# Forgetting attention: the value product with 64 leading and 64 low columns in one stationary operand

## The chip, the cores and the metric

The kernel runs on one core of one Trainium2 chip. The metric is device microseconds (us) of one execution. TensorE does matrix products and transposes, VectorE (DVE) and ScalarE (ACT) do elementwise work and read PSUM, GpSimd (POOL) does elementwise work in SBUF, SyncE (SP) issues transfers. Each engine works through its own queue in order; semaphores tie the queues together.

## The reference

Two transformer blocks in float32 over 512 tokens (plus 16 meta tokens in the first, plus 256 context tokens in the second). The change touches one piece of the first block, the forgetting attention (8 heads of 64):

```
c = jnp.cumsum(log_f, axis=1)                       # per head
s = q . k / sqrt(64) + (c_i - c_j);  causal mask     # blocks of 128 queries, 528 keys
p = softmax(s)
o = einsum('bhqk,bkhd->bqhd', p, v)                  # the value product
```

In the same block runs a linear recurrence (HGRN2) of 4 heads with 128 keys, evaluated in levels of halved block size; the outputs of both are concatenated and multiplied by `w_out`. Then come a feed-forward network, a block of differential attention, a block of neighbourhood attention, and a feed-forward network behind each.

## The kernel before

Float32 operands go to TensorE in the type float32r, and accuracy is kept by splitting: `hi` is the operand rounded to that type, `lo` the rest, and every product is three, `hi*hi + hi*lo + lo*hi`. The helper `mm3` (lines 367 to 371) issues them; `halve_scalar` (L534, on ACT) writes `hi` from the source and `halve_vector` (L539, on DVE) writes `lo = source - hi` behind it. Weights come in chunks: SP fetches one into `raw`, ACT rounds it to `whi` (`split_hi`, L400), POOL or DVE makes `wlo` (`split_lo`, L411), and TensorE uses it.

The stage that holds the change is "mixers", from about 60 to 373 us of the span. `mixers_steps` is a hand-written list of steps: for each of four rounds j, attention for the pair of heads 2j and 2j+1 and recurrence head j. In a round there are four query blocks i = 0 to 3, each with "scores" and two "turn" steps (transposes of the probabilities, one per head). "values" steps exist for x = 2, 3 (query blocks 0 and 1, head 0 and head 1 of the pair) and x = 6, 7 (blocks 2 and 3): 16 in all. Between them the list is filled with the projections of the next round and with the recurrence ("level", "keys", "states", "output", "sums"). TensorE runs the steps in list order. The orders of ACT, DVE and POOL come from `in_time`: each step has a planned end on TensorE (`mixers_cost`, `mixers_chain`), the tables `MIXERS_SCALAR`, `MIXERS_VECTOR` and `MIXERS_GPSIMD` give each part of a step a lateness against it, and the parts are sorted by the resulting time. `Spare` picks for each result the PSUM bank (4 to 7) planned free first; TensorE waits there for the last reader of the bank's former content.

A "values" step: the stationary operand is `vh` or `vl`, 128 keys by 128 columns (both heads of the pair, 64 each); the moving operand is the transposed probabilities of one head, `th`/`tl` (blocks of keys) and `mh`/`ml` (the 16 meta keys), 256 query columns, 128 in the diagonal block. For x = 2, 3 there are 3 blocks (256, 128 and 256 columns), for x = 6, 7 five (three of 256, one of 128, one of 256). Of the 128 rows that come out, the 64 of the head (rows `r` to `r+63`) are used: ACT rounds them to `foh` ("o_hi"), DVE writes `fol` ("o_lo"), which frees the bank.

ACT's order around x = 6, 7 of round j is: gk_root (L1281, L1283), o_hi 6, o_hi 7, tv_hi of the next round (two pieces), split (L400), decay (L1287), exp (L1229), gv (L1292), t_hi, share (L1235), gv second half (L1292), split, gtv (L1297, L1299), level_exp (L1313). DVE's is: o_lo 6, gk_close (L1460 to L1468, five instructions), o_lo 7, max (L1410), tv_lo, decay_sum (L1473, five scans), inv (L1416), t_lo, diff (L1491, L1492), scaled (L1499, L1500). TensorE transposes the evacuated gv (L1098) behind both halves of L1292, and then runs the level products (L1114).

At the end of the stage, ACT has "close", split, o_hi 6, o_hi 7, DVE has "close", "part" 7 (L1551), o_lo 6, o_lo 7, and `mixed_tensor` begins with a wait on the o_lo of x = 7 and the recurrence's close.

## Time and profile before

| | |
|---|---|
| median of 3 runs | 2616.43 us |
| all three | 2621.54, 2616.43, 2616.13 us |
| span of the profiled execution | 2620.7 us |
| TensorE busy | 2449.5 us, 93% |
| VectorE, ScalarE, GpSimd busy | 1563.9, 1056.3, 345.6 us |
| stage "mixers" | about 60 to 373 us |

The profile comes from one execution, whose own time is known as its span, 2620.7 us from the first to the last instruction; no other figure was taken for it. It lies 4.3 us above the median of the three runs and 0.8 us below the slowest. In the rows below PE is TensorE's products and PEld its weight loads; L534 means line 534 of the kernel before.

### The profile page before, as it was taken

To read this page: it belongs to the slowest core of one execution; us is meant where nothing else is said; L and a number is where in the kernel's file an instruction comes from. 1 tells how busy PE (TensorE), PEld (TensorE's weight loads), DVE (VectorE), ACT (ScalarE), POOL (GpSimd) and SP (SyncE) were. 2 spreads that over 40 slices of the span, in tenths; PEclk is the share of its full clock that TensorE was granted. 3 is DMA by queue.
4 is the path that set the end of the run, shared out by engine and by line. 5 is a ranking of instruction groups with operands and counts; after the bars stand their busy time and mean duration, and the time that the engine had idled before them with its cause. 6 is when DMAs were issued, how large, how long until landed. Compare 5 with 4: busy or idle time off the path is not lost.

```text
span 2620.7 us, 35948 instructions
## 1 busy us (share of the span) xinstructions
PE 2449.5 (93%) x14115; PEld 2107.4 (80%) x14115; DVE 1563.9 (60%) x3020; ACT 1056.3 (40%) x1878; POOL 345.6 (13%) x241
## 2 busy tenths in 40 slices
PE   7999989999998999998899999999889897999998
PEld 6788877788787878776788888889778786888887
DVE  4566657878867777777756544445545456533334
ACT  5455534223254555555521211113555545422223
POOL 2222210000031221221000000002222322000001
PEclk9999999999999999999899999999999999899999
DMA  4222125555521111111234333331212122232331
GB/s 121 61 65 58 47 83 160 174 157 176 175 75 43 41 35 39 41 33 41 73 104 130 104 110 108 119 115 46 53 44 57 45 53 57 76 109 85 100 109 49
DMA packets 240617, 220.73 MB, mean 84 GB/s; under 512 B 26620, under 2 KB 207650, under 8 KB 240450
## 3 DMA queue, kind: packets, MB, share of 16 engines
q1 hardware_dynamic: 240450, 218.45, 27.4%
q8 instruction: 112, 1.84, 0.3%
q14 instruction: 55, 0.45, 0.1%
HBM read 216.17 MB, written 2.24 MB: 83 GB/s over the span
## 4 chain that ended last, share of the span: by engine, by line
PE 73%; DVE 13%; ACT 7%; issue 5%; DMA 1%; SPq 0%; POOL 0%; DVEq 0%; POOLq 0%; ACTq 0%
PE ps L369 23%; PE ps L370 22%; PE ps L371 22%; ACT whi L400 1%; PE ps L2492 1%; DVE FR L539 1%; PE ps L2944 1%; ACT FA L2585 1%; DVE FA L673 1%; DVE hT L2665 1%; ACT FR L534 1%; DVE wlo L411 1%; DVE FA L2705 1%; PE ps L1114 1%; ACT FA L3013 1%
## 5 line engine op out<-in xcount | busy, mean ns | idle before, releaser
L369 PE MATMUL ps<-Uh,whi 128*128 128x512 f32 (+2 forms) x2544 | 898.3, 353 | 17.5 <-ACT FA L2604 5.9
L370 PE MATMUL ps<-Ul,whi 128*128 128x512 f32 (+2 forms) x2544 | 884.5, 348 | 0.0
L371 PE MATMUL ps<-Uh,wlo 128*128 128x512 f32 (+2 forms) x2544 | 883.7, 347 | 0.0
L369 PEld LDWEIGHTS ps<-Uh,whi 128*128 128x128 f32 x2544 | 487.5, 192 | 84.7 <-issue 18.0
L371 PEld LDWEIGHTS ps<-Uh,wlo 128*128 128x128 f32 x2544 | 486.3, 191 | 59.5
L370 PEld LDWEIGHTS ps<-Ul,whi 128*128 128x128 f32 x2544 | 487.2, 192 | 57.0
L400 ACT ACTIVATE whi<-raw 128x1024 fp32r<-128x1024 f32 (+3 forms) x211 | 297.8, 1411 | 539.8 <-PE ps L371 539.6
L411 DVE TENSOR_TENSOR wlo<-raw,whi 128x2048 fp32r<-128x2048 f32 (+2 forms) x117 | 239.3, 2046 | 258.5 <-ACT whi L400 258.1
L369 PE MATMUL ps<-FR,whi 128*128 128x512 f32 (+1 forms) x864 | 302.4, 350 | 14.3 <-DVE FR L539 7.8
L411 POOL TENSOR_TENSOR wlo<-raw,whi 128x1024 fp32r<-128x1024 f32 (+1 forms) x94 | 227.3, 2418 | 666.3 <-ACT whi L400 665.5
L370 PE MATMUL ps<-FR,whi 128*128 128x512 f32 (+1 forms) x864 | 298.6, 346 | 0.0
L371 PE MATMUL ps<-FR,wlo 128*128 128x512 f32 (+1 forms) x864 | 298.3, 345 | 0.0
L539 DVE TENSOR_TENSOR FR<-ps,FR 128x512 fp32r<-128x512 f32 (+7 forms) x284 | 142.6, 534 | 141.5 <-ACT FR L534 140.7
L2185 POOL TENSOR_TENSOR FA<-FA 128x256 f32<-128x256 f32 x63 | 48.5, 787 | 1298.6 <-ACT FA L2065 1297.5
L534 ACT ACTIVATE FR<-FA 128x512 fp32r<-128x512 f32 x100 | 58.4, 584 | 352.1 <-DVE FA L1860 343.5
L673 DVE SCALAR_TENSOR_TENSOR FA<-FA,cond 128x512 f32<-128x512 f32 x280 | 197.0, 745 | 2.6 <-DMA FA<-in_ada_w_dram 1.2
L369 PEld LDWEIGHTS ps<-FR,whi 128*128 128x128 f32 x864 | 164.4, 190 | 38.0 <-issue 9.6
L534 ACT ACTIVATE FR<-ps 128x512 fp32r<-128x512 f32 (+7 forms) x304 | 131.5, 467 | 125.2 <-PE ps L371 74.3
L371 PEld LDWEIGHTS ps<-FR,wlo 128*128 128x128 f32 x864 | 164.3, 190 | 20.0
L370 PEld LDWEIGHTS ps<-FR,whi 128*128 128x128 f32 x864 | 164.5, 190 | 19.3
L369 PE MATMUL ps<-whi 128*128 128x512 f32 (+1 forms) x208 | 86.8, 417 | 47.4 <-DVE hT L3097 28.5
L1860 DVE TENSOR_TENSOR FA<-ps,FA 128x512 f32<-128x512 f32 x88 | 54.9, 623 | 115.9 <-PE ps L371 114.4
(347 smaller groups left out, 2999.2 us busy)
## 6 DMA issues: line engine op xcount, KB each, us to landing
FA<-in_ada_w_dram SPq DMA_DIRECT2D x192, 256.0 KB, 2.8
raw<-in_ffn_w_gate_up_dram SPq DMA_DIRECT2D x44, 1024.0 KB, 5.1
raw<-in_ffn_w_down_dram SPq DMA_DIRECT2D x24, 768.0 KB, 4.6
raw<-in_w_in_dram SPq DMA_DIRECT2D x29, 512.0 KB, 3.9
raw<-in_da_wqkv_dram SPq DMA_DIRECT2D x24, 512.0 KB, 3.7
raw<-in_na_wqkv_dram SPq DMA_DIRECT2D x24, 512.0 KB, 3.8
raw<-in_w_ffn_gate_dram SPq DMA_DIRECT2D x11, 1024.0 KB, 5.4
raw<-in_w_ffn_up_dram SPq DMA_DIRECT2D x11, 1024.0 KB, 5.4
```

The costliest lines, as they stand in the source:

```text
L369: e.matmul(out, ah, bh, start=start, stop=False)
L370: e.matmul(out, ah, bl, start=False, stop=False)
L371: return e.matmul(out, al, bh, start=False, stop=stop)
L400: e.activation(K.view(K.hi[i % 2], i), K.view(K.raw[i % 2], i), ACT.Copy).then_inc(*K.ev("whi", i))
L411: e.tensor_tensor(K.view(K.lo[i % 2], i), K.view(K.raw[i % 2], i), K.view(K.hi[i % 2], i).bitcast(F32), ALU.subtract).then_inc(*K.ev(by, i))
L534: e.activation(hi, src, ACT.Copy, scale=scale).then_inc(*K.ev(*done))
L539: e.tensor_tensor(lo, src, hi.bitcast(F32), ALU.subtract).then_inc(*K.ev(*done))
L673: e.scalar_tensor_tensor(out=o, in0=wv, scalar=K.cond[:, k, c:c + 1], in1=o, op0=ALU.mult, op1=ALU.add).then_inc(*K.ev("ada", i, c))
L1114: t = e.matmul(o[:, c * P:(c + 1) * P], a[:, c * P:(c + 1) * P], b[:, c * P:(c + 1) * P], start=True, stop=True)
L1860: e.tensor_tensor(mt, K.bank(4 + m % 2)[:, 0:t1 - t0], K.sil[:, m % 2, 0:t1 - t0], ALU.mult).then_inc(*K.ev("f_mul", st, m))
L2185: e.tensor_tensor(acc, acc, K.st_sq4[:, k, :], ALU.add).then_inc(*K.ev("pool_sum", f.st, n, i, z))
L2492: t = e.matmul(K.ps[:, 1024 * mp + c0:1024 * mp + c0 + a1 - a0], q[r:r + 64, q0:q0 + P], k[r:r + 64, a0:a1], start=n == 0, stop=n == 2)
```

## The change

The leading and the low part of one head's values stand side by side as one stationary operand of 128 columns (64 and 64), and each block takes two products (with the leading and the low probabilities) instead of three. The rows that come out are 64 sums of the leading values and 64 of the low ones, and they have to be added: ACT copies the low rows to the head's partitions in SBUF ("o_other"), DVE adds the others from PSUM ("o_sum", which now frees the bank), and o_hi and o_lo then read this sum in SBUF. The planned times of o_hi and o_lo move by 1.0 us. `tv_hi` and `tv_lo` write the new layout; `Uh` and `Ul` become halves of one tensor `U` so that one pattern reaches both.

```diff
-        self.fv = self.Uh[:, 0:5, 528:656], self.Ul[:, 0:5, 528:656]
+        zy = self.U[:, :, 528:656].rearrange("p (z y) d -> p z y d", z=2)[:, :, 0:5, :]
+        self.fvw, self.fv = [zy[:, h, :, :] for h in range(2)], (zy[:, :, :, 0:64], zy[:, :, :, 64:128])
+        self.folow, self.fofull = self.hT[:, 0:4, 560:624], self.hT[:, 4:8, 560:624]
...
+def by_64(a):
+    return a.rearrange("p (a b) -> p a b", b=64)
+def by_pair(a):
+    return a.rearrange("p (y h d) -> p h y d", h=2, d=64)
...
-        o = K.hold(w, b, ("x_o_lo", j, x))
+        o = K.hold(w, b, ("x_o_sum", j, x))
...
-            t = mm3(e, o[:, c0:256], vh[0:kn, y, :], vl[0:kn, y, :], ah, al, z == 0, z == len(order) - 1)
+            for m, a in enumerate((th[:, y, c0:256], tl[:, y, c0:256]) if y < 4 else (mh[0:NM, :], ml[0:NM, :])):
+                t = e.matmul(o[:, c0:256], K.fvw[h][0:kn, y, :], a, start=z == 0 and m == 0, stop=z == len(order) - 1 and m == 1)
...
-                 "values": (("o_hi", 0.1),),
+                 "values": (("o_other", 0.1), ("o_hi", 1.1)),
...
-        halve_scalar(K, e, K.bank(K.xbank["tv", j, 0]).rearrange("p (a b) -> p a b", a=4), vh[:, 0:4, :], ("x_tv_hi", j, 0))
+        halve_scalar(K, e, by_pair(K.bank(K.xbank["tv", j, 0])), vh[:, :, 0:4, :], ("x_tv_hi", j, 0))
...
     elif what == "o_hi":
         r, c0 = 64 * (x % 2), (x // 4) * 256
+        w.wait_ge(*K.at("x_o_sum", j, x))
+        halve_scalar(K, e, K.fofull[r:r + 64, :, :], by_64(K.foh[r:r + 64, j, c0:c0 + 256]), ("x_o_hi", j, x))
+    elif what == "o_other":
+        r = 64 * (x % 2)
         w.wait_ge(*K.at("x_values", j, x))
-        halve_scalar(K, e, K.bank(K.xbank["o", j, x])[r:r + 64, 0:256], K.foh[r:r + 64, j, c0:c0 + 256], ("x_o_hi", j, x))
+        n = 4 * j + x // 4 * 2 + x % 2 - 2
+        if n >= 0:
+            w.wait_ge(*K.at("x_o_sum", n // 4, 2 + 4 * (n % 4 // 2) + n % 2))
+        e.activation(K.folow[r:r + 64, :, :], by_64(K.bank(K.xbank["o", j, x])[64 - r:128 - r, 0:256]), ACT.Copy).then_inc(*K.ev("x_o_other", j, x))
...
-                 "turn": (("t_lo", 0.8),), "values": (("o_lo", 0.6),),
+                 "turn": (("t_lo", 0.8),), "values": (("o_sum", 0.6), ("o_lo", 1.6)),
...
+    elif what == "o_sum":
+        r, n = 64 * (x % 2), 4 * j + x // 4 * 2 + x % 2 - 2
+        w.wait_ge(*K.at("x_o_other", j, x))
+        if n >= 0:
+            w.wait_ge(*K.at("x_o_lo", n // 4, 2 + 4 * (n % 4 // 2) + n % 2))
+        e.tensor_tensor(K.fofull[r:r + 64, :, :], by_64(K.bank(K.xbank["o", j, x])[r:r + 64, 0:256]), K.folow[r:r + 64, :, :], ALU.add).then_inc(
+            *K.ev("x_o_sum", j, x))
```

The orders that follow from the new tables, by the sorting of `in_time`: ACT around x = 6, 7: gk_root, o_other 6, o_hi 6, o_other 7, tv_hi, o_hi 7, split, decay. DVE: o_sum 6, gk_close, o_lo 6, o_sum 7, max, o_lo 7, tv_lo, decay_sum. ACT around x = 2, 3 (rounds 0 to 2): o_other 2, share, o_hi 2, o_other 3, t_hi, o_hi 3, split. ACT at the end: close, split, o_other 6, o_hi 6, o_other 7, o_hi 7; DVE: close, part 7, o_sum 6, o_lo 6, o_sum 7, o_lo 7.

## Rows read from the trace of the kernel before

**Rows 1.** Page: the span and the engines' busy time.
```profile
span 2620.7 us, 35948 instructions
PE 2449.5 (93%) x14115; PEld 2107.4 (80%) x14115; DVE 1563.9 (60%) x3020; ACT 1056.3 (40%) x1878; POOL 345.6 (13%) x241
```
**Rows 2.** Waits of TensorE in 60 to 380 us: us in total, times, longest.
```profile
PE ps L1114 <- DVE raw L1500: 7.0, 10, 0.9
```
**Rows 3.** Timeline of TensorE: values 2, 3 of round 0; start, us, instruction.
```profile
109.42 0.28 PE L370 MATMUL ps<-wlo,Uh 128*128 128x256 f32 x1
109.54 0.28 PE L371 MATMUL ps<-whi,Ul 128*128 128x256 f32 x1
...
111.96 0.66 PE L1064 MATMUL ps<-ident,FA 128*128 128x128 f32 x4
```
**Rows 4.** Timeline of TensorE: values 6, 7 of round 3.
```profile
365.20 0.28 PE L369 MATMUL ps<-whi,Uh 128*128 128x256 f32 x1
...
367.19 0.39 PE L369 MATMUL ps<-FR,Uh 128*128 128x256 f32 x1
```
**Rows 5.** Timeline of ACT: around values 2, 3 of round 0.
```profile
110.69 0.38 ACT L534 ACTIVATE FR<-ps 64x256 fp32r<-64x256 f32 x1 [1.58 <-PE ps L371]
110.97 1.35 ACT L1235 ACTIVATE FA<-FA,stat 128x528 f32<-128x528 f32 x2
```
**Rows 6.** Timeline of ACT: around values 6, 7 of round 0.
```profile
145.75 0.38 ACT L534 ACTIVATE FR<-ps 64x256 fp32r<-64x256 f32 x1 [1.26 <-PE ps L371]
146.33 0.75 ACT L534 ACTIVATE Uh<-ps 128x512 fp32r<-128x512 f32 x2 [0.20 <-PE ps L1034]
146.98 1.04 ACT L400 ACTIVATE whi<-raw 128x1024 fp32r<-128x1024 f32 x1
148.06 0.65 ACT L1287 ACTIVATE FA<-raw 128x528 f32<-128x528 f32 x1
...
151.96 0.94 ACT L1235 ACTIVATE FA<-FA,stat 128x272 f32<-128x272 f32 x2 [0.94 <-DVE stat L1416]
153.47 0.39 ACT L1292 ACTIVATE FA<-ps 128x264 f32<-128x264 f32 x1 [0.56 <-PE ps L371]
```
**Rows 7.** Timeline of DVE: the same stretch.
```profile
148.00 0.43 DVE L539 TENSOR_TENSOR FR<-ps,FR 64x256 fp32r<-64x256 f32 x1
...
149.98 1.89 DVE L1473 TENSOR_TENSOR_SCAN FA<-ones,FA 128x128 f32<-128x128 f32 x5
...
156.08 1.54 DVE L1499 TENSOR_TENSOR raw<-raw,FA 128x256 f32<-128x256 f32 x1 [3.04 <-ACT raw L1313]
```
**Rows 8.** Timeline of POOL: the same stretch.
```profile
148.16 2.40 POOL L411 TENSOR_TENSOR wlo<-raw,whi 128x1024 fp32r<-128x1024 f32 x1 [9.19 <-ACT whi L400]
154.95 2.39 POOL L411 TENSOR_TENSOR wlo<-raw,whi 128x1024 fp32r<-128x1024 f32 x1 [4.38 <-ACT whi L400]
```
**Rows 9.** Timeline of TensorE: the transposes of gv behind both halves of L1292.
```profile
153.91 0.66 PE L1098 MATMUL ps<-ident,FA 128*128 128x128 f32 x4 [0.48 <-ACT FA L1292]
```
**Rows 10.** The scans of line 1473: ns min/median/max.
```profile
L1473 DVE TENSOR_TENSOR_SCAN FA<-ones,FA x15: 157/393/860, 150.0 to 301.7; 128x128 f32<-128x128 f32 x12, 128x16 f32<-128x16 f32 x3
```
**Rows 11.** Timeline, all engines: the end of the stage.
```profile
370.88 0.76 ACT L534 ACTIVATE FR<-ps 64x256 fp32r<-64x256 f32 x2
...
371.62 0.68 DVE L1551 TENSOR_TENSOR hT<-ps,hT 128x512 f32<-128x512 f32 x1
...
372.22 0.86 DVE L539 TENSOR_TENSOR FR<-ps,FR 64x256 fp32r<-64x256 f32 x2
...
373.29 0.77 PE L369 MATMUL ps<-FR,whi 128*128 128x512 f32 x1 [3.97 <-DVE FR L539]
```
**Rows 12.** Timeline of TensorE: an idle time of 3.12 us later on.
```profile
395.44 0.47 PE L369 MATMUL ps<-Uh,whi 128*128 128x512 f32 x1 [3.12 <-ACT hT L1674]
```
**Rows 13.** Windows: busy us of PE, PEld, DVE, ACT, POOL; then TensorE's clock.
```profile
396.00:398.00 2.00, 2.00 (x7) 1.62 (x6) 1.93 (x4) 1.54 (x5) 0.00 (x0) 0.62 0.34 117
398.00:400.00 2.00, 2.00 (x6) 1.52 (x6) 1.92 (x3) 2.00 (x3) 0.00 (x0) 0.52 0.00 0
```

More of the change, by code:

```diff
@@ L1075, in fox_tensor @@
             kn = P if y < 4 else NM
-            ah, al = (th[:, y, c0:256], tl[:, y, c0:256]) if y < 4 else (mh[0:NM, :], ml[0:NM, :])
-            t = mm3(e, o[:, c0:256], vh[0:kn, y, :], vl[0:kn, y, :], ah, al, z == 0, z == len(order) - 1)
+            for m, a in enumerate((th[:, y, c0:256], tl[:, y, c0:256]) if y < 4 else (mh[0:NM, :], ml[0:NM, :])):
+                t = e.matmul(o[:, c0:256], K.fvw[h][0:kn, y, :], a, start=z == 0 and m == 0, stop=z == len(order) - 1 and m == 1)
         t.then_inc(*K.ev("x_values", j, x))
@@ L1219, in fox_scalar @@
         w.wait_ge(*K.at("x_tv", j, 0))
-        halve_scalar(K, e, K.bank(K.xbank["tv", j, 0]).rearrange("p (a b) -> p a b", a=4), vh[:, 0:4, :], ("x_tv_hi", j, 0))
+        halve_scalar(K, e, by_pair(K.bank(K.xbank["tv", j, 0])), vh[:, :, 0:4, :], ("x_tv_hi", j, 0))
         w.wait_ge(*K.at("x_tv", j, 1))
-        halve_scalar(K, e, K.bank(K.xbank["tv", j, 1])[0:NM, 0:P], vh[0:NM, 4, :], ("x_tv_hi", j, 1))
+        halve_scalar(K, e, by_pair(K.bank(K.xbank["tv", j, 1])[0:NM, 0:P])[:, :, 0, :], vh[0:NM, :, 4, :], ("x_tv_hi", j, 1))
     elif what == "exp":
@@ L1397, in fox_vector @@
         w.wait_ge(*K.at("x_tv_hi", j, 0))
-        halve_vector(K, e, K.bank(K.xbank["tv", j, 0]).rearrange("p (a b) -> p a b", a=4), vh[:, 0:4, :], vl[:, 0:4, :],
-                     ("x_tv_lo", j, 0))
+        halve_vector(K, e, by_pair(K.bank(K.xbank["tv", j, 0])), vh[:, :, 0:4, :], vl[:, :, 0:4, :], ("x_tv_lo", j, 0))
         w.wait_ge(*K.at("x_tv_hi", j, 1))
-        halve_vector(K, e, K.bank(K.xbank["tv", j, 1])[0:NM, 0:P], vh[0:NM, 4, :], vl[0:NM, 4, :], ("x_tv_lo", j, 1))
+        halve_vector(K, e, by_pair(K.bank(K.xbank["tv", j, 1])[0:NM, 0:P])[:, :, 0, :], vh[0:NM, :, 4, :], vl[0:NM, :, 4, :], ("x_tv_lo", j, 1))
     elif what == "max":
@@ L1434, in fox_vector @@
         w.wait_ge(*K.at("x_o_hi", j, x))
-        halve_vector(K, e, K.bank(K.xbank["o", j, x])[r:r + 64, 0:256], K.foh[r:r + 64, j, c0:c0 + 256],
-                     K.fol[r:r + 64, j, c0:c0 + 256], ("x_o_lo", j, x))
+        halve_vector(K, e, K.fofull[r:r + 64, :, :], by_64(K.foh[r:r + 64, j, c0:c0 + 256]),
+                     by_64(K.fol[r:r + 64, j, c0:c0 + 256]), ("x_o_lo", j, x))
+    elif what == "o_sum":
[5 more added lines that the diff above has]
+            *K.ev("x_o_sum", j, x))
 def hgrn_vector(K, e, w, what, h, n):
@@ L3274, in build @@
         m["hT"] = sb("hT", [P, KC, 768])
-        m["Uh"] = sb("Uh", [P, KC, 768], F32R)
-        m["Ul"] = sb("Ul", [P, KC, 768], F32R)
+        m["U"] = sb("U", [P, 2 * KC, 768], F32R)
+        m["Uh"], m["Ul"] = m["U"][:, 0:KC, :], m["U"][:, KC:2 * KC, :]
         m["FR"] = sb("FR", [P, 13376], F32R)
```

## Prediction

> **What bounds the kernel now.** I read the page first, then the waits of TensorE in the stage that the change touches, then the timelines of each engine around the value products. The page shows TensorE at work for 93% of the span [rows 1]; DVE has 60% and ACT 40%. Taken alone that says that fewer products are less time. In the stage itself, though, TensorE is held up at fixed places: ten times for the recurrence's level inputs from DVE (7.0 us in all, [rows 2]) and in each round for ACT's evacuation of gv [rows 9]. What counts is whether a saved product lies behind such a place or ahead of it, and what the new steps do to the two in-order queues of ACT and DVE.
>
> **What is removed on TensorE.** 16 values steps: eight (x = 2, 3) lose 3 products each, eight (x = 6, 7) lose 5: 64 products. Products of 256 columns start 0.12 us apart [rows 3]: 64 x 0.12 = 7.7 us. From above: a head's whole step of 15 products lasts 1.99 us [rows 4], 0.133 each, 8.5 us for 64. I take 7.7: per pair of steps 0.7 us at x = 2, 3 and 1.2 us at x = 6, 7. The weight loads go with the products, and the two that stay have the same form as before.
>
> **x = 2, 3 (four places).** The new ACT order is o_other 2, share, o_hi 2, o_other 3, t_hi. o_other 2 takes the slot of the old o_hi (0.38 us at 110.69, [rows 5]), 0.35 us earlier; share, which takes 1.35 us for two heads, then starts at about 110.63 instead of 110.97, and its first half is done at 111.3. The next transposes on TensorE, at 111.96 [rows 3], need it: they could start at 111.26 for the saved products and at 111.35 for share. So 0.6 us is gained. Behind it t_hi comes in ACT's queue behind share and two operations of 0.38 us, where one stood before, but these start earlier: 112.65 against 112.74. In round 3 share has run before and the whole 0.7 us is gained. Sum: 3 x 0.6 + 0.7 = 2.5 us gained. From below: if o_hi 2 held ACT for a whole DVE operation (0.43 us, [rows 7]) at each place, 4 x 0.43 = 1.7 us of it would go; from above 2.8 us.
>
> **x = 6, 7 at the turn of a round (three places).** Here the sorted orders clash. DVE: o_sum 6, gk_close (five operations), o_lo 6, o_sum 7, max, o_lo 7. ACT: o_other 6, o_hi 6, o_other 7, tv_hi, o_hi 7, split, decay. o_hi used to wait for TensorE alone; the old o_hi 7 ran at 145.75 [rows 6], and its o_lo stood until 148.00 behind gk_close on DVE [rows 7], which held up nobody. Now o_hi 7 waits for o_sum 7, which stands behind gk_close and o_lo 6. Step by step, with the times of round 0:
> - o_sum 6 takes the slot of the old o_lo 6, so gk_close ends as before; o_lo 6 starts at 148.00, o_sum 7 about 0.35 us later and ends at 148.78.
> - ACT is through with tv_hi at 146.4 and stands until 148.8; o_hi 7 ends at 149.2. Behind it are queued the split (old 146.98), decay (old 148.06), exp, both halves of gv, share. The split starts at 149.15, 2.2 us late.
> - decay runs at 150.2 to 150.85, so DVE's five scans can start at 150.85 instead of 149.98. But POOL starts its part of the same chunk behind the split, at 150.3 instead of 148.16, and has 2.40 us [rows 8], to 152.7.
> - Here the port matters. In the old trace the first scan meets the end of POOL's operation: it takes 860 ns where the median is 393 [rows 10], and ends 0.28 us after POOL (149.98 + 0.86 = 150.84 against 150.56). L1499, 256 columns, begun at 156.08 inside POOL's next operation (154.95 to 157.34), takes 1.54 us and also ends 0.28 us after it [rows 7, 8]. So the scans, which read two SBUF operands, wait for POOL: the first ends at 153.0. The old five ended 1.03 us after the first (149.98 + 1.89 = 151.87); the new end at 154.0, 2.2 us late.
> - inv and then share follow: share at about 154.1 instead of 151.96, and behind its 0.94 us the second half of gv at 155.0 instead of 153.47 [rows 6], 1.55 us late. TensorE transposes gv behind it [rows 9], and the level products come behind that.
>
> TensorE's own gain of 1.2 us is spent waiting here, and 1.55 us is added. The other two turns run the same pattern 75 and 150 us later; by the same steps, with POOL at 225.5 and 300.5 us, they come to 1.65 and 1.9 us. Sum: 5.1 us lost. The lower bound is that scans and POOL don't meet: then decay's delay is eaten by ACT's idle time (0.94 and 0.56 us in [rows 6]) down to about 0.2 us a turn. Below that, if ACT weren't held at all, 1.2 us a turn would be gained. The upper bound is ACT's whole delay of 2.2 us plus a POOL operation in the way of the level inputs, 1.3 us (the excess of L1499): 3.5 us a turn.
>
> The port is also what the Trainium skill names: "GPSIMD Engine Reference", section "Specifications", says that GpSimd's SBUF interfaces are shared with VectorE and contend with its instructions that have two SBUF inputs. The trace agrees, with the 860 and 1540 ns above. By that rule the new o_lo, which reads its sum from SBUF and no more from PSUM, is exposed as well; at x = 3 it would fall under POOL's operation. This changes the sum little, since the next DVE operation there is held by the same POOL operation already.
>
> SP fetches the chunk after the next once POOL is done, here 2.2 us later; ACT's split that needs it comes some ten us on, so this is hidden. If it weren't, each turn would cost the 2.2 us. The turn step of the next round takes the bank of x = 7, free at 148.78, when TensorE gets there at 149.0: just in time.
>
> **The end of the stage.** The last o_lo lets `mixed_tensor` begin. Now: two o_hi on ACT from 370.88, DVE's part 7 at 371.62, two o_lo from 372.22, TensorE at 373.29 after 3.97 us idle [rows 11]. The saved 1.2 us of products lie in that idle time, so nothing is gained. New chain from 372.22: o_sum 6 (0.43), o_hi 6 (0.38), o_other 7 (0.38, behind it on ACT), o_sum 7 (0.43), o_hi 7 (0.38), o_lo 7 (0.43), with 0.03 us between engines: done at 374.72 where it was 373.08. Cost 1.65 us. From below 0.43 us (only one more operation on the path), from above 2.5 us (each of the five hand-overs takes the 0.21 us between the last o_lo and TensorE, instead of 0.03).
>
> **The clock.** Each turn leaves TensorE idle for about 3.1 us (152.3 to 155.4). In the old trace an idle time of 3.12 us [rows 12] is followed by a granted clock of 0.62 and 0.52 in two windows of 2 us [rows 13]: (0.38 + 0.48) x 2 / 0.5 = 3.4 us at 1.2 GHz instead of 2.4, 1.7 us of work lost. Part falls into later waits for level inputs, up to 0.9 us each [rows 2]. I take 0.7 a turn, 2.1 us; bounds 0 and 1.7 a turn. At the end of the stage the clock is low after the idle time already.
>
> **Other edits.** The new layout in tv_hi and tv_lo moves the same elements; 0, with 0.1 us for each of eight operations as a bound. 16 more ACT operations of 0.38 us (6 us) and 16 more of DVE of 0.43 us (7 us) lie, apart from the places above, in idle time of engines that are busy for 60% at most. If that cover were gone, they would cost 13 us. No transfer is added.
>
> **Sum.** -2.5 + 5.1 + 1.65 + 2.1 = +6.35 us, on a profiled span of 2620.7 us: 2627.0. The median of the runs is 4.3 us below that span, and I carry the difference over to it: 2616.4 + 6.4 = 2622.8 us.
>
> **Rivals.**
> 1. The products decide (faster). ACT recovers its delay in each turn and TensorE keeps what it saves: -7.7 us, of which 1.2 lies in the idle time at the end, plus 1.65 there and 0.3 for share: -4.55, so 2611.9 us; where a stretch of low clock in a round also falls away, 1.7 us less. For it speaks 93% on TensorE; against it that ACT's decay is what DVE waits for, and DVE what ACT's share waits for. Chance 0.16.
> 2. The hold on ACT is real, but scans and POOL don't meet, because the split, and POOL with it, comes half an operation earlier or later: -2.5 + 3 x 0.2 + 1.65 = -0.25, so 2616.2 us, no change. Against it speaks that the split and decay stand side by side in one queue, so that POOL and the scans start within 0.6 us of each other. Chance 0.22.
> 3. The low clock lasts twice as long in each turn, as after the 3.97 us of idle time at the end of the stage. It decides where the idle time in a turn goes above about 3.5 us: 3 x 1.7 = 5.1 us on top and the bound of the clock term: 2616.4 + 6.4 + 5.1 = 2628 to 2631 us. Chance 0.08.
> My forecast has 0.54, with a range of its own of 2618 to 2628 us (the clock term at its ends, -2.1 and +3, and 1 to 2 us for the turns).
>
> **How the numbers follow.** A measurement of this kernel can tell about 0.2%, 5.2 us. Of my forecast's 0.54 I put 0.37 above +5.2 us and 0.17 within; rival 3 is above, rival 2 within, rival 1 is below with 0.10 (with such a stretch gone) and within with 0.06. Slower 0.45, the same 0.45, faster 0.10. The range of 2613 to 2629 us leaves out most of rival 1 and part of rival 3.
>
> **What would show it.** Right: at each turn an L534 on ACT that waits over 2 us for DVE, the split behind it over 2 us late against tv_hi, the first scan over 1.5 us long, TensorE idle for about 3 us ahead of L1098, and a low clock in the windows after; at the end 1.6 us more from DVE's part 7 to TensorE's start. Wrong: scans of 393 ns, or the turns of the rounds no longer than before; then the time is at or under the old one.

## The result and the profile after

The changed kernel takes 2627.0 us (median of 7 runs, 2626.4 to 2631.2) beside 2618.3 us for the kernel before (7 runs, 2615.7 to 2624.4). The ratio is 1.0035 with a 95% interval of 1.0024 to 1.0046: slower by 6 to 12 us. The same pair once more, in the runs of experiment 1, gave 1.0021 (1.0013 to 1.0030). 64 matmuls fewer, and the kernel is slower. Two executions that took far longer than all others (6180 and 3734 us) are left out of every median and ratio here.

The page first: span, and instructions by engine. TensorE has the 64 matmuls less and 6 us less work than in [rows 1]; ACT and DVE have 16 operations more each.

```profile
span 2625.2 us, 35866 instructions
PE 2443.2 (93%) x14051; PEld 2100.1 (80%) x14051; DVE 1579.6 (60%) x3036; ACT 1061.5 (40%) x1894; POOL 345.3 (13%) x241
```

The waits of TensorE from 60 to 385 us show where the time is: us in total, times, longest.

```profile
PE ps L1124 <- DVE raw L1524: 11.3, 14, 1.6
PE ps L371 <- DVE FR L541: 7.7, 2, 6.9
PE ps L1108 <- ACT FA L1310: 5.6, 4, 3.2
PE ps L371 <- DVE U L541: 3.2, 2, 1.7
```

The level inputs cost 11.3 us in 14 waits where [rows 2] had 7.0 in 10; the longest idle time, at the end of the stage, is 6.9 us where [rows 11] had 3.97.

**A turn of a round.** ACT at the first turn (start, us, instruction, idle time ahead of it and who ended it), against [rows 6]:

```profile
146.86 0.41 ACT L536 ACTIVATE FR<-hT 64x256 fp32r<-64x256 f32 x1 [2.23 <-DVE hT L1459]
147.30 1.06 ACT L402 ACTIVATE whi<-raw 128x1024 fp32r<-128x1024 f32 x1
148.26 0.63 ACT L1305 ACTIVATE FA<-raw 128x528 f32<-128x528 f32 x1
...
152.27 0.93 ACT L1245 ACTIVATE FA<-FA,stat 128x272 f32<-128x272 f32 x2 [1.79 <-DVE stat L1433]
153.11 0.37 ACT L1310 ACTIVATE FA<-ps 128x264 f32<-128x264 f32 x1
```

The hold is the first line: `o_hi` 7 follows 2.23 us of waiting for DVE's `o_sum` 7 (2.24 us in each of the other two turns), and the split (L402) and the decay (L1305) are behind it in the queue. DVE and POOL in the same stretch, against [rows 7, 8]:

```profile
146.40 0.43 DVE L1459 TENSOR_TENSOR hT<-ps,hT 64x256 f32<-64x256 f32 x1
...
148.15 0.88 DVE L541 TENSOR_TENSOR U<-ps,U 128x512 fp32r<-128x512 f32 x2
148.96 3.22 DVE L1497 TENSOR_TENSOR_SCAN FA<-ones,FA 128x128 f32<-128x128 f32 x5
```

```profile
148.50 2.38 POOL L413 TENSOR_TENSOR wlo<-raw,whi 128x1024 fp32r<-128x1024 f32 x1 [11.58 <-ACT whi L402]
```

The five scans take 3.22 us instead of 1.89 (3.23 in the other two turns), and end at 152.18, 1.3 us behind POOL's operation (150.88), where [rows 7, 8] had 151.87 and 150.56: the first stands for POOL, as the prediction had it. TensorE stands twice in this turn:

```profile
148.90 0.39 PE L371 MATMUL ps<-U,whi 128*128 128x264 f32 x1 [1.52 <-DVE U L541]
...
153.53 0.66 PE L1108 MATMUL ps<-ident,FA 128*128 128x128 f32 x4 [1.44 <-ACT FA L1310]
```

The first of the two, for the low part of the turned values (`tv_lo`, L541 at 148.15 on DVE), whose PSUM bank TensorE needs, the prediction didn't have. It lies ahead of the second and shortens it; together they are the 3 us that were forecast in one piece. The second turn has 1.70 and 0.48 us; the third has no wait for `tv_lo` and the whole idle time in one piece, as forecast:

```profile
305.00 0.55 PE L1108 MATMUL ps<-ident,FA 128*128 128x128 f32 x3 [3.25 <-ACT FA L1310]
```

**x = 3.** What the prediction took for a gain. In round 0, DVE, POOL and TensorE:

```profile
114.99 2.19 DVE L541 TENSOR_TENSOR FR<-hT,FR 64x256 fp32r<-64x256 f32 x1
114.50 2.39 POOL L413 TENSOR_TENSOR wlo<-raw,whi 128x1024 fp32r<-128x1024 f32 x1 [11.37 <-ACT whi L402]
119.58 1.13 PE L1124 MATMUL ps<-raw 128*128 128x128 f32 x8 [0.94 <-DVE raw L1524]
```

`o_lo` 3 reads its sum from SBUF and starts 0.49 us into POOL's operation. It takes 2.19 us instead of 0.42, the level inputs' operations stand behind it, and TensorE waits 0.94 us where it did not wait before. In the kernel before it was the first of these operations that met POOL there, and it lost less:

```profile
115.82 1.31 DVE L1491 TENSOR_TENSOR raw<-FA 128x256 f32<-128x256 f32 x1
```

Rounds 1 and 2 of the changed kernel have the same 2.19 us. In round 3 the two operations start within 10 ns of each other:

```profile
345.47 2.11 DVE L541 TENSOR_TENSOR FR<-hT,FR 64x256 fp32r<-64x256 f32 x1
345.46 1.84 POOL L413 TENSOR_TENSOR wlo<-raw,whi 128x768 fp32r<-128x768 f32 x1 [4.50 <-ACT whi L402]
351.32 1.13 PE L1124 MATMUL ps<-raw 128*128 128x128 f32 x8 [1.58 <-DVE raw L1524]
```

**The end of the stage**, all engines, against [rows 11]:

```profile
375.67 0.68 DVE L1575 TENSOR_TENSOR hT<-ps,hT 128x512 f32<-128x512 f32 x1
376.27 0.40 DVE L1459 TENSOR_TENSOR hT<-ps,hT 64x256 f32<-64x256 f32 x1
376.70 0.42 ACT L536 ACTIVATE FR<-hT 64x256 fp32r<-64x256 f32 x1 [1.28 <-DVE hT L1459]
377.60 0.43 DVE L1459 TENSOR_TENSOR hT<-ps,hT 64x256 f32<-64x256 f32 x1
378.06 0.41 ACT L536 ACTIVATE FR<-hT 64x256 fp32r<-64x256 f32 x1 [0.54 <-DVE hT L1459]
378.51 0.42 DVE L541 TENSOR_TENSOR FR<-hT,FR 64x256 fp32r<-64x256 f32 x1 [0.48 <-ACT FR L536]
379.14 0.76 PE L371 MATMUL ps<-FR,whi 128*128 128x512 f32 x1 [6.92 <-DVE FR L541]
```

From DVE's part 7 (375.67) to TensorE's start it is 3.47 us, where it was 373.29 - 371.62 = 1.67: 1.80 us more.

**The clock.** Two windows of after (the number behind the five engines is the granted clock), and one of before:

```profile
226.00:228.00 2.00, 2.00 (x11) 2.00 (x10) 2.00 (x10) 0.38 (x1) 0.22 (x1) 0.50 0.20 39
307.00:309.00 2.00, 2.00 (x7) 1.52 (x6) 1.91 (x4) 0.06 (x1) 1.29 (x1) 0.50 0.02 4
```

```profile
114.00:116.00 2.00, 2.00 (x7) 1.61 (x7) 1.59 (x6) 0.33 (x1) 1.53 (x1) 0.50 0.00 0
```

The granted clock is at its lower level, 1.2 GHz (0.50), for some 3.4 us each time. The changed kernel has two such stretches in its rounds. One lies in the second turn, behind the wait of 1.70 us for `tv_lo`; the other begins at 307 us, 2 us behind the 3.25 us of idle time of the third turn. The kernel before has three, one in each of the rounds 0 to 2 (from 113, 188 and 263 us) behind the values of x = 2, 3, where the longest wait of TensorE in the 20 us ahead was 0.94 us. A trace is one execution, and two executions of one kernel differ in this (the trace here has two more stretches ahead of the rounds, at 41 and 69 us, that of experiment 1 none there), so these stretches must be told apart from the engines' waits before two traces are compared.

That is done by landmarks: the time of TensorE's first transposes for the turned values (turn begins), of its transposes of gv (turn ends, and the next round begins), of the norm sums in round 3, and of the first output product. The table has, for each piece, how much longer it is than in one and the same trace, that of the kernel before with a wait on POOL (experiment 5), which has no stretch at 1.2 GHz in the rounds. What lies ahead of the first transposes of gv and behind the first output product is not in it: the two traces of the changed kernel differ there by 1.6 and 2.5 us.

```
us more than the reference    round 0  turn 1  round 1  turn 2  round 2  turn 3  round 3   end
kernel before                  +1.61   +0.01   +1.66   +0.01   +1.53    0.00   -0.02  -0.01
changed kernel                 -1.09   +2.83   -0.99   +3.69   -1.08   +3.27   +2.72  +1.79
changed kernel, again (1)      -1.08   +2.85   -0.98   +3.70   -1.10   +3.23   +1.12  +1.80
products only (2)              -1.80   +4.49   -1.80   +4.53   -1.87   +2.48   -0.67  -0.01
additions only (3)             +0.40   +1.71   +0.51   +1.81   +0.44   +2.15   +1.36  +1.81
direct (4)                     -1.78   +5.42   -1.79   +6.33   -1.84   +4.45   -0.70  +0.91
products, POOL waits (6)       -1.80   +0.82   -1.47   +1.14   -1.76   +0.40   -0.68   0.00
changed, POOL waits (7)        -1.09   +1.86   -1.00   +2.16   -1.05   +1.44   -0.36  +1.80
direct, POOL waits (8)         -1.85   +1.86   -1.55   +3.70   -1.83   +1.47   -0.69  +0.91
hold only (9)                  +0.02   +1.47   +0.01   +1.53   -0.02   +1.84   +1.02   0.00
as 7, and at x = 3 (10)        -0.65   +1.87   -0.55   +2.17   -0.62   +1.43   +1.44  +1.79
as 8, tv_lo earlier (11)       -1.83   +1.15   -0.46   +1.45   -1.58   +1.42   -0.69  +0.91
as 11, end reordered (12)      -1.77   +1.13   -0.44   +1.44   -1.58   +1.44   -0.71  +0.32
```

The three +1.6 of the kernel before are its three stretches at 1.2 GHz. The row of the changed kernel adds up to +11.1, that of the kernel before to +4.8: 6.35 us more. Of this the stretches of low clock are -4.8 + 1.6 (round 3) + about 0.8 (turn 2, an estimate: it is 0.86 us longer than turn 1) = -2.4, and the engines' waiting and work +8.75.

Other rows hold such stretches too, and they must be read with them: turn 2 of experiment 1, turns 1 and 2 of 2 (150 to 153 and 225 to 228 us), all three turns of 4, turn 2 of 8 (224 to 227 us), and round 3 of 1, 3, 9 and 10 (from 305, 305, 302 and 307 us). Experiments 5, 6, 7, 11 and 12 have none in the rounds and turns.

### The profile page after: what moved, and what is told of

Its sections match the earlier page's. It is cut to its first block, busy times and chain, and to the rows that moved or that the text cites. A ratio compares the mean times of both kernels' runs of the same rounds, so it can differ in the third digit from the quotient of the medians.

```text
span 2625.2 us, 35866 instructions
## 1 busy us (share of the span) xinstructions
PE 2443.2 (93%) x14051; PEld 2100.1 (80%) x14051; DVE 1579.6 (60%) x3036; ACT 1061.5 (40%) x1894; POOL 345.3 (13%) x241
## 3 DMA queue, kind: packets, MB, share of 16 engines
q8 instruction: 112, 1.84, 0.3%
HBM read 216.17 MB, written 2.24 MB: 83 GB/s over the span
## 4 chain that ended last, share of the span: by engine, by line
PE 69%; DVE 16%; ACT 9%; issue 5%; SPq 0%; DMA 0%; POOL 0%; DVEq 0%; POOLq 0%; ACTq 0%
PE ps L371 21%; PE ps L372 21%; PE ps L373 21%; DVE FR L541 2%; ACT whi L402 1%; PE ps L2516 1%; ACT FA L2609 1%; ACT FR L536 1%; PE ps L2968 1%; DVE FA L675 1%; DVE hT L2689 1%; PE ps L1124 1%; DVE FA L2729 1%; DVE wlo L413 1%; ACT FA L3037 1%
## 5 line engine op out<-in xcount | busy, mean ns | idle before, releaser
L371 PE MATMUL ps<-U,whi 128*128 128x512 f32 (+2 forms) x2544 | 900.2, 354 | 20.9 <-ACT FA L2628 5.9
L372 PE MATMUL ps<-U,whi 128*128 128x512 f32 (+2 forms) x2544 | 886.4, 348 | 0.0
L373 PE MATMUL ps<-U,wlo 128*128 128x512 f32 (+2 forms) x2544 | 885.6, 348 | 0.0
L371 PEld LDWEIGHTS ps<-U,whi 128*128 128x128 f32 x2544 | 488.1, 192 | 88.8 <-issue 18.1
L373 PEld LDWEIGHTS ps<-U,wlo 128*128 128x128 f32 x2544 | 487.5, 192 | 59.7
L372 PEld LDWEIGHTS ps<-U,whi 128*128 128x128 f32 x2544 | 488.2, 192 | 57.0
L402 ACT ACTIVATE whi<-raw 128x1024 fp32r<-128x1024 f32 (+3 forms) x211 | 297.9, 1412 | 538.9 <-PE ps L373 538.6
L541 DVE TENSOR_TENSOR FR<-ps,FR 128x512 fp32r<-128x512 f32 (+5 forms) x268 | 135.7, 540 | 129.7 <-ACT FR L536 129.2
L536 ACT ACTIVATE FR<-ps 128x512 fp32r<-128x512 f32 (+5 forms) x288 | 125.1, 472 | 115.2 <-PE ps L373 66.7
```

The lines of the kernel that those rows point to most:

```text
L371: e.matmul(out, ah, bh, start=start, stop=False)
L372: e.matmul(out, ah, bl, start=False, stop=False)
L373: return e.matmul(out, al, bh, start=False, stop=stop)
L402: e.activation(K.view(K.hi[i % 2], i), K.view(K.raw[i % 2], i), ACT.Copy).then_inc(*K.ev("whi", i))
L536: e.activation(hi, src, ACT.Copy, scale=scale).then_inc(*K.ev(*done))
L541: e.tensor_tensor(lo, src, hi.bitcast(F32), ALU.subtract).then_inc(*K.ev(*done))
```

## The experiments

Experiments 1 to 4 share a chip and the runs of the kernel before (2619.15 us, 30 runs), so do 5 to 8 (2617.2, 34 runs) and 9 to 12 (2618.62, 35 runs). The ratio behind each time is that to the kernel before beside it. In the edits, `...` marks what is left out.

**1. The changed kernel again**, unedited.

> The changed kernel once more, beside the next three on one chip. Hold theory (ACT stands at each turn of a round for o_sum 7, POOL and DVE's scans meet behind it, the end of the stage has a longer chain): +5 to +9 us against before, with the scans over 3 us long at three turns. Clock theory (the +9 us of the medians are the luck of where the low clock falls): the difference moves by several us from chip to chip and may be 0.

Measured: 2626.46 us, 1.0021 (1.0013 to 1.0030). The slowdown is there again. In the table its trace differs from the first in one piece, round 3: the same two instructions, 10 ns apart as before, end the other way round.

```profile
343.75 0.42 DVE L541 TENSOR_TENSOR FR<-hT,FR 64x256 fp32r<-64x256 f32 x1
343.74 2.12 POOL L413 TENSOR_TENSOR wlo<-raw,whi 128x768 fp32r<-128x768 f32 x1 [4.49 <-ACT whi L402]
```

Now DVE isn't held (0.42 us) and POOL is (2.12 us for 1.84), and round 3 is 1.12 in the table where it was 2.72: 1.6 us hang on who comes first.

**2. The products alone.** The kernel before, with the third product of each block left out (low values by leading probabilities are missing in the result); nothing else.

```diff
-            t = mm3(e, o[:, c0:256], vh[0:kn, y, :], vl[0:kn, y, :], ah, al, z == 0, z == len(order) - 1)
+            e.matmul(o[:, c0:256], vh[0:kn, y, :], ah, start=z == 0, stop=False)
+            t = e.matmul(o[:, c0:256], vh[0:kn, y, :], al, start=False, stop=z == len(order) - 1)
```

> The kernel before with the third product of each block (low values times leading probabilities) left out and nothing else: 64 products fewer, orders and waits as before. Hold theory: TensorE is the bound where nothing new waits, so 4 x 0.7 + 3 x 1.15 = 6.3 us less, the 1.2 us at the end of the stage hidden in the idle time there. Rival (TensorE waits for the level chain anyway, so products are worth little): 0 to 3 us less.

Measured: 2621.97 us, 1.0008 (0.9999 to 1.0016). Even without one new step the saved products bring nothing. TensorE's own gain is there in full (-1.80 a round), and each turn gives back 2.5 to 4.5 us. The 2.5 us of turn 3 are waits alone; in turns 1 and 2 some 2 us more lie in a stretch at 1.2 GHz that follows the waits. The cause of the waits is new. Against DVE's chain ACT's split comes 1.1 us earlier, POOL's operation behind it too, and this now falls into the closing of g_k on DVE:

```profile
144.19 2.59 DVE L1468 TENSOR_SCALAR raw<-raw 128x528 f32<-128x528 f32 x1
...
147.21 0.43 DVE L539 TENSOR_TENSOR FR<-ps,FR 64x256 fp32r<-64x256 f32 x1
```

```profile
144.10 2.38 POOL L411 TENSOR_TENSOR wlo<-raw,whi 128x1024 fp32r<-128x1024 f32 x1 [8.06 <-ACT whi L400]
```

L1468 takes 0.43 us where it doesn't meet POOL. `o_lo` 7 is behind it, TensorE needs its bank, and stands:

```profile
147.78 0.41 PE L1064 MATMUL ps<-ident,FA 128*128 128x128 f32 x2 [1.56 <-DVE FR L539]
149.13 0.39 PE L369 MATMUL ps<-Uh,whi 128*128 128x264 f32 x1 [0.94 <-DVE Ul L539]
```

**3. The additions alone.** The changed kernel with a third product, the second one done twice (the low probabilities count double in the result), so that TensorE's work is that of before.

```diff
-            for m, a in enumerate((th[:, y, c0:256], tl[:, y, c0:256]) if y < 4 else (mh[0:NM, :], ml[0:NM, :])):
+            for m, a in enumerate((th[:, y, c0:256], tl[:, y, c0:256], tl[:, y, c0:256]) if y < 4 else (mh[0:NM, :], ml[0:NM, :], ml[0:NM, :])):
...
```

> The changed kernel with the product of the low probabilities issued twice in each block, so 64 products more and all the adding as it is. Hold theory: at x = 6, 7 the product time lies in TensorE's idle time of 3 us, so only the four places of x = 2, 3 count: 2.8 us more than the changed kernel, +8 to +12 against before. Rival (both sides simply add up): 7.7 us more than the changed kernel, +13 to +17 against before.

Measured: 2628.96 us, 1.0033 (1.0022 to 1.0044). That is 2.5 us above the changed kernel (2626.46), near the 2.8 of the hold theory and far from its rival's 7.7. In the table the turns take 1.71, 1.81 and 2.15 us: 1.12 us less than in the changed kernel (turn 1), while the rounds take 1.5 us more. So of the products, those of x = 6, 7 (1.14 us) are worth nothing to the changed kernel, since they only make TensorE reach the hold sooner.

**4. Direct.** Two products a block, but without the hand-over between ACT and DVE: ACT rounds the leading rows from PSUM, and DVE subtracts the rounded part and adds the other half of the rows, both from PSUM.

```diff
...
-                 "values": (("o_other", 0.1), ("o_hi", 1.1)),
+                 "values": (("o_hi", 0.1),),
...
-                 "turn": (("t_lo", 0.8),), "values": (("o_sum", 0.6), ("o_lo", 1.6)),
+                 "turn": (("t_lo", 0.8),), "values": (("o_lo", 0.6),),
...
+        e.tensor_tensor(rest, by_64(o[r:r + 64, 0:256]), by_64(K.foh[r:r + 64, j, c0:c0 + 256]).bitcast(F32), ALU.subtract).then_inc(
...
+        e.tensor_tensor(by_64(K.fol[r:r + 64, j, c0:c0 + 256]), by_64(o[64 - r:128 - r, 0:256]), rest, ALU.add).then_inc(
...
```

> The two products kept, the adding done without a hand-over between ACT and DVE: ACT rounds the leading rows from PSUM as in the kernel before, DVE subtracts them and then adds the low rows, both operations with one PSUM operand (the first writes to the partitions of the low rows). Hold theory: ACT never stands, no operation of the new ones reads two SBUF operands, the scans take 1.7 us as before: -6.3 + 0.8 at the end of the stage = 5.5 us less than before. Rival (the added elementwise work is what costs, 16 operations of 0.4 us on DVE): 0 to 4 us more than before.

Measured: 2624.73 us, 1.0020 (1.0011 to 1.0030): a miss. The hand-over is gone, and the split is early again: POOL meets the closing of g_k, as in experiment 2, and TensorE stands 2.51 us for the bank of `o_lo` 7. (The lines are of turn 1; in turns 2 and 3 POOL meets the instruction ahead of this one, L1479, which takes 2.89 us instead of 0.77.)

```profile
146.66 2.48 DVE L1482 TENSOR_SCALAR raw<-raw 128x528 f32<-128x528 f32 x1
```

```profile
150.61 0.41 PE L1074 MATMUL ps<-ident,FA 128*128 128x128 f32 x2 [2.51 <-DVE FR L1450]
```

So the next four keep POOL out of the way by one wait, and nothing else: at the three turns its operation starts when DVE has done the scans.

```diff
+            if x == "gv" and j:
+                w.wait_ge(*K.at("g_sum", j))
             w.wait_ge(*K.at(*K.pool_prev))
```

**5. The kernel before with this wait.**

> The kernel before; at the three turns of a round POOL's part of the split waits until DVE's scans are done. Port theory (the price at the turns is POOL's operation standing in the way of DVE's operations with two SBUF operands or in a two-port mode): the kernel before is timed so that POOL just misses gk_close, so little is to be had: the first scan of 860 ns goes, 0 to 1 us less. Rival (a later weight part on POOL holds up TensorE): 1 us or more above before.

Measured: 2616.84 us, 0.9996 (0.9987 to 1.0006). The wait costs and brings nothing there; it can be used as a probe. POOL's operation is itself held by DVE's next ones then (3.33 us instead of 2.40 at the first turn), and no wait of TensorE comes of it.

**6. The products alone, with the wait.**

> As e2 (third product left out), and POOL waits for the scans at the three turns. Port theory: in e2 the split on ACT came 1.2 us earlier, POOL met gk_close (L1468 at 2.59 us instead of 0.43), and this took the gain of the products back; without the meeting 5 to 6.5 us less than before. Rival (TensorE waits for the level chain in any case): as e2, +1 to +3 us.

Measured: 2610.74 us, 0.9974 (0.9964 to 0.9983), 6.5 us faster than before. The turns give back 0.82, 1.14 and 0.40 us instead of 4.49, 4.53 and 2.48. Turn 3, which has no stretch of low clock in either trace, shows the waits alone, 2.1 us; in turns 1 and 2 the stretches of experiment 2 are gone as well. This one wait brings the gain back, so it had been lost to POOL meeting DVE. (For how much of the 6.5 us this stands, see the clock below.)

**7. The changed kernel with the wait.**

> The changed kernel, and POOL waits for the scans at the three turns. Port theory: the scans take 1.5 us instead of 3.2 while ACT still stands for o_sum 7, so some 1.5 us a turn come back: 4 to 5 us less than the changed kernel, +1 to +3 us against before. Rival (ACT's standing is the price, not the port): as the changed kernel.

Measured: 2620.49 us, 1.0009 (0.9998 to 1.0019). The scans take 1.43 us again, and the turns fall from 2.83, 3.69 and 3.27 to 1.86, 2.16 and 1.44, by 1.0, 1.5 and 1.8 us, where 1.5 was expected. Turns 1 and 3, without low clock in either trace, give the price of the meeting: 1.0 and 1.8 us. Beside experiment 6, which saves the same products under the same wait but has no hold, each turn is 1.0 us longer (1.04, 1.02, 1.04): the price of the hold without the meeting. Less the 1.14 us that the saved products of x = 6, 7 bring ahead of it, a turn is 0.7, 1.0 and 0.3 us longer than in the kernel before. In turn 1 TensorE now stands 1.52 us for `tv_lo` and only 0.48 for gv, as long as in the kernel before: `tv_lo` is behind `o_lo` 7 on DVE, and this behind the held `o_hi` 7.

**8. Direct, with the wait.**

> As e4 (adding on DVE from PSUM, no hand-over), and POOL waits for the scans at the three turns. Port theory: in e4 L1482 of gk_close met POOL (2.48 us); without it the gain of the products is kept, less 0.8 us at the end of the stage: 4 to 6 us less than before. Rival (the added DVE work is the price): as e4, +4 to +6 us.

Measured: 2617.36 us, 0.9993 (0.9984 to 1.0003): better than experiment 4, but 4 to 6 us less than before was expected. g_k is closed undisturbed, but the turns still lose 1.86, 3.70 and 1.47 us (the second with a stretch of low clock in it). The timeline of TensorE in turn 1 says on what:

```profile
148.71 0.41 PE L1074 MATMUL ps<-ident,FA 128*128 128x128 f32 x2 [0.45 <-DVE FR L1450]
150.07 0.39 PE L371 MATMUL ps<-U,whi 128*128 128x264 f32 x1 [0.94 <-DVE U L541]
```

Both are DVE's, and both stand there behind the closing of g_k: the bank of part 7, and `tv_lo`.

**9. The hold alone.** The kernel before with all its products and additions as they were; only ScalarE's `o_hi` 7 waits, at the three turns, for DVE's closing of g_k.

```diff
         w.wait_ge(*K.at("x_values", j, x))
+        if x == 7 and j < 3:
+            w.wait_ge(*K.at("g_k", j + 1))
```

> The kernel before, with one change: at the three turns ScalarE's rounding of the leading rows (part 7 of rounds 0 to 2) waits until VectorE has closed g_k of the next round, as the hand-over makes it do in the changed kernel. All arithmetic and all products stay as before. My theory: the split starts about 1.3 us later, POOL's first operation then runs into the scans, the decays and the second half of the gate's values come 0.6 to 0.7 us later at each turn, and the kernel becomes 1 to 4 us slower, ratio 1.0005 to 1.0015. The rival (ScalarE's order has slack at the turn, and the hand-over there costs only what the missing products take): no change, ratio 0.9995 to 1.0004, with TensorE's wait for the gate's transposes as in the kernel before.

Measured: 2624.34 us, 1.0017 (1.0007 to 1.0027): slower by 2 to 7 us, 4.4 by the ratio, a little more than the 1 to 4 us expected. TensorE's wait for gv goes from 1.7 us in the kernel before to

```profile
PE ps L1098 <- ACT FA L1294: 5.9, 4, 2.1
```

and the turns take 1.47, 1.53 and 1.84 us more. All of it comes from one more wait, three times, on an engine that is busy for 40%. It is the price of the hold with what follows from it, not of the hold by itself: POOL's operation starts later and meets the scans here too:

```profile
147.19 3.28 DVE L1475 TENSOR_TENSOR_SCAN FA<-ones,FA 128x128 f32<-128x128 f32 x5 [0.20 <-ACT FA L1289]
```

**10. As 7, and POOL also waits at x = 3** for `o_lo` 3.

```diff
...
+            if x == "gate" and j < 3 or x == "part" and parts == 5:
+                w.wait_ge(*K.at("x_o_lo", j, 3))
```

> The changed kernel; POOL's split of the low columns waits for VectorE's scans at the three turns, and the one behind part 3 waits for VectorE's rounding of part 3, so that neither can start beside it. Theory (a race of some 10 ns in round 3, worth 1.6 us when POOL wins it, is what spreads the changed kernel's runs): the rounding of part 3 takes 0.42 us in each round, and the time is that of the variant with the wait at the turns alone (2620.5) less 0.3 to 1.3 us, with less spread. Rival (what is held there is hidden, or the split that then comes later costs as much): the same time as that variant, 2620.5, or up to 1 us more.

Measured: 2621.45 us, 1.0012 (1.0001 to 1.0023): no gain, and the spread isn't less (2618.1 to 2630.1). `o_lo` 3 takes 0.42 us everywhere now, but POOL's operation, 1.0 us later against TensorE, falls on the next one, which TensorE needs just as much:

```profile
118.16 2.61 DVE L1516 TENSOR_TENSOR raw<-FA 128x256 f32<-128x256 f32 x1
```

```profile
122.38 1.13 PE L1124 MATMUL ps<-raw 128*128 128x128 f32 x8 [1.38 <-DVE raw L1524]
```

Rounds 0 to 2 lose 0.44 us more than in 7. My idea that the contest in round 3 makes the spread of the runs falls with it.

**11. As 8, with `tv_lo` ahead of the running maximum** on DVE instead of behind it.

```diff
...
-                 "fk": (("k_lo", 0.8),), "turn_fv": (("tv_lo", 0.9),), "scores": (("max", 0.1), ("inv", 3.2)),
+                 "fk": (("k_lo", 0.8),), "turn_fv": (("tv_lo", 0.6),), "scores": (("max", 0.1), ("inv", 3.2)),
...
```

> Two products a block, ScalarE and VectorE each reading the product themselves, POOL's split waiting for the scans, and VectorE's rounding of the low columns for the turn's second half placed ahead of the running maximum instead of behind the closing of g_k. Theory (at the turn TensorE now waits for this rounding, 1.1 us): that wait goes, and the time falls by 0.8 us a turn, 2.4 in all, against 2618.9 of the variant without it: about 2616, ratio to the kernel before 0.998 to 0.999. Rival (the scans end later by the 0.9 us that went ahead of them, and the gate's values with them): 2618.9 or 1 us more, and the wait stands at the gate's transposes instead.

Measured: 2613.53 us, 0.9982 (0.9972 to 0.9991). That is below the 2616 that were expected; the clock (below) has a part in it. Turn 1 falls from 1.86 to 1.15 us, TensorE's wait of 0.94 us for `tv_lo` to 0.22. Something is still lost there: behind turn 1 POOL's two operations now stand back to back and hold two of DVE's for the level inputs (L1506 and L1507, 2.28 and 2.61 us instead of 0.4), TensorE waits 1.04 us for these, and round 1 is -0.46 in the table where 8 has -1.55.

**12. As 11, and DVE's part 7 at the end of the stage stands behind `o_lo` 7.**

```diff
...
-        elif what == "part":
...
+        elif what == "part" and x < KC - 1:
+            add_part(x)
         fox_vector(K, e, w, what, j, x)
         hgrn_vector(K, e, w, what, j, x)
+    add_part(KC - 1)
```

> As the one before, and at the end of the stage VectorE's addition to the head's sum for part 7 stands behind the rounding of its low rows, not ahead of it. Theory: the last output product starts 0.6 us earlier, 0.6 us less in all. Rival (the chain ends in something else there): no change from the one before.

Measured: 2613.42 us, 0.9977 (0.9965 to 0.9989). The piece at the end is 0.32 us instead of 0.91, the 0.6 us expected; the two times can't be told apart. It is the fastest kernel here with the whole computation, 5 us under the kernel before.

## Why the prediction was right, point by point

The forecast was 2622.8 us on a median of 2616.4, +6.4; measured is +8.7 with an interval of +6 to +12, and in the second set of runs +3.4 to +8. The sign, the place and the mechanism held; two terms of the sum were wrong, in opposite directions.

- **The hold on ACT: right.** The prediction has ACT standing from 146.4 to 148.8, 2.4 us; it stands 2.23 us in front of `o_hi` 7. What the hold and the meeting behind it add to a turn, over the lost gain of the products, was forecast as 1.55, 1.65 and 1.9 us. The changed kernel gives 1.69, about 1.8 (without the low clock) and 2.13; experiment 9, which has all its products and a hold of its own (till g_k is closed, with `tv_hi` behind it), 1.47, 1.53 and 1.84.
- **The scans meet POOL: right**, 3.22 us for the five instead of 1.89. Experiment 7 shows by taking the meeting away that it is 1.0 us of turn 1 and 1.8 of turn 3. With the saved products lost as well the first turn was to cost 2.75 us; it cost 2.83. The second rival was right that without the meeting little would be added, though 0.3 to 1.0 us a turn and not 0.2, but the two do meet.
- **What the turn step waits for was incomplete, at little cost.** The bank of x = 7 is free in time, but TensorE stands 1.52 us for `tv_lo` in turn 1 and 1.70 in turn 2, since `tv_lo` stands behind gk_close, max and `o_lo` 7 on DVE. I had followed ACT's queue and the bank of x = 7 only. The wait lies ahead of the one for gv and comes off it. So the sign that I had named, idle time of about 3 us ahead of L1098 at each turn, came in turn 3 alone (3.25 us). In experiments 7 and 8, where the later wait is short, the one for `tv_lo` is the one that counts.
- **x = 2, 3: the first step that failed.** Forecast -2.5 us. The products' 0.7 us is there in each round (experiment 6: -1.80 = -0.7 - 1.1), and the changed kernel has 0.71 us less of it (-1.09). The cause is the sentence on `o_lo` at x = 3 under POOL's operation, which "changes the sum little, since the next DVE operation there is held by the same POOL operation already". That one was held, but `o_lo`'s own 0.42 us came on top, everything behind it was later, and the next operations had no slack: TensorE waits 0.94 us. In round 3, where the two start together, it is 1.6 us or nothing. The term is +1.4 us in the first trace and -0.1 in the second (the rounds of the table, less 1.14 for x = 6, 7 in rounds 0 to 2, and round 3 less its stretch of low clock of 1.6 and 1.5), instead of -2.5.
- **The end of the stage: right.** 1.65 us forecast, 1.80 measured, in all of experiments 1, 3, 7 and 10. (The steps listed in the prediction add up to 374.77 and not to its 374.72, 1.69 us.)
- **The clock: the second step that failed, wrong in sign.** Forecast +2.1 us, one stretch of low clock behind each turn. The first turn's 3 us of idle time, in two pieces, had none behind it; the second turn had one, about 0.8 us of cost since it runs partly into time that TensorE would have waited anyway; the third, idle for 3.25 us in one piece, had one behind it, 1.6 us. So what the change adds is near the forecast (2.4 us). What the prediction put at nothing, though its first rival names it, is what the change takes away: the three stretches of the kernel before, 4.8 us in its trace, are gone. In this pair of traces the term is -2.4 us. Over all runs of experiment 1 the mean granted clock of the changed kernel is 0.0007 +- 0.0011 above that of before (11 and 30 runs): no difference that can be told. Why the kernel before has its three stretches no run shows; the trace of experiment 5, the same kernel but for POOL's wait, has none.

Summed: +1.4 (x = 2, 3) + 5.6 (turns: 2.83, 2.9 without the low clock, and 3.27, each less 1.14) + 1.8 (end) - 2.4 (clock) = +6.4, beside +6.35 in the landmarks and +6.35 in the forecast. The agreement is luck in part: an error of 3.9 us at x = 2, 3 stands against one of 4.5 us in the clock. Of the rivals, the first (the products decide) is refuted by experiment 2, in a way it did not name: the products alone bring nothing either.

## What to carry to other kernels

Before you save work on the busiest engine, ask what its consumers do earlier and whom they then meet. Here 64 matmuls fewer brought nothing by themselves, since POOL's operation came 1.1 us earlier and held DVE; one wait that keeps it off was worth about 9 us with the saved products (1.0008 against 0.9974; in the table 8.7 us, of which some 4 are stretches of low clock) and nothing without them. A hand-over to an in-order queue is priced by what is queued behind it and whom this then meets, as in experiment 9, not by its own 0.4 us. And a stall that "is held anyway" must be followed one operation further: what comes in front of it adds its own length to all that follows.

## What the hardware showed that I had not expected

**Who comes first holds the other, and it works both ways.** In a pair of experiment 1 DVE keeps its 0.42 us and POOL takes 2.12 instead of 1.84; in the first trace POOL keeps 1.84 and DVE takes 2.11, on recorded starts that are 10 ns apart in the same order in both. So such a start in the record doesn't say who won; the durations do. The Trainium skill, "SBUF — State Buffer", section "Who interferes with whom", says of the ports that the two engines share that whoever issues first gets the pair for the whole instruction and the other blocks fully; the durations of these two traces agree. The same section counts `tensor_scalar` among the operations that can take the pair, and the 2.59 and 2.48 us of L1468 and L1482 (0.43 alone, fp32) bear that out. The blocked DVE operation ends 0.28 us behind POOL in round 3 of the first trace (347.58 against 347.30), as in [rows 7, 8].

**The granted clock differs between kernels by as much as the edits are worth.** The mean over all runs, less that of the kernel before beside them (with two standard errors):

```
changed kernel, again (1)  +0.0007 +- 0.0011
products only (2)          +0.0003 +- 0.0016
additions only (3)         -0.0020 +- 0.0018
direct (4)                 +0.0013 +- 0.0011
before, POOL waits (5)     -0.0005 +- 0.0015
products, POOL waits (6)   +0.0019 +- 0.0012
changed, POOL waits (7)    +0.0009 +- 0.0016
direct, POOL waits (8)     +0.0016 +- 0.0015
hold only (9)              -0.0003 +- 0.0015
as 7, and at x = 3 (10)    +0.0018 +- 0.0014
as 8, tv_lo earlier (11)   +0.0027 +- 0.0012
as 11, end reordered (12)  +0.0027 +- 0.0013
```

0.0027 of 2613 us is 7 us, more than the 5 to 6 us by which kernel 12 is faster. In the landmarks kernel 12 adds up to -0.2 us and kernel 6 to -3.4 us against the reference, which has no stretch of low clock, and the kernel before to +4.8, which is its three stretches. Behind the first output product, where nothing was edited, the trace of 12 is 3.6 us shorter than that of the kernel before (2243.8 against 2247.4). So the times of 6, 11 and 12 are shown to be shorter, and the meeting at the turn is shown to be gone, but most of 11's and 12's gain over the kernel before lies in a better clock, in part inside the edited stage and in part behind it. Each of these is one trace, and two traces of the changed kernel differ by 2.5 us behind the stage. Why the better clock is granted was not tried and stays open.
